# A diffusion-transformer step: the filler matmuls of the delta-rule scan redistributed, an activation reload split into four awaited groups, and the down-projection's operand loads cut into pieces

## The chip, the cores and the metric

The kernel runs on one core of one Trainium2 chip. The metric is the device time in microseconds (us) of one execution. Three executions of the kernel before gave 2773.88, 2765.34 and 2752.76 us, median 2765.34 us.

## The reference

One trunk layer of a hybrid backbone, in float32, for 256 context tokens and 1024 latent tokens (1280 together, `T`), width 1024:

- `h = RMSNorm(x) * g * (1 + scale) + shift`, with shift, scale and gate from `SiLU(cond) @ w_ada + b_ada`.
- The in-projection `h @ w_in` (1024 to 4896 columns) gives attention q, k, v, the inputs of a gated delta net (q, k, v, z, beta, alpha) and two gates.
- Attention: 8 query heads, 2 key heads, softmax over context, cached and latent keys.
- Delta net: conv, SiLU, then for each of 8 heads a forward and a backward scan in chunks: `S_t = a_t (I - b_t k_t k_t^T) S_{t-1} + b_t k_t v_t^T`, `o_t = S_t^T q_t`. In a chunk a triangular matrix is inverted.
- `x = x + gate1 * W_o(sig(ga) * W_pa(attention) + sig(gb) * W_pb(delta))`.
- `x = x + gate2 * W_down(SiLU(h2 @ W_gate) * (h2 @ W_up))`, with 2816 hidden columns.

Every output is compared in float32, so each large product is made of three matmuls on a high and a low part of both factors: high·high, low·high and high·low.

## The kernel before, in words

The program is a sequence of blocks, one after the other, each with a hand-written order for every engine and with semaphores between the engines: modulation and norm, in-projection, delta scan, keys, attention, merge, and feed-forward. The change touches the delta scan and the last part of the feed-forward.

**Delta scan (`delta_scan`, line 751).** A unit is one chunk of 128 tokens in one direction. Units 0 to 19 alternate forward and backward. The loop runs over u from -3 to 20: in step u the engines invert unit u's matrix, carry the state of unit u-1, and prepare units u+1 to u+3. Below, "unit u" is the stretch of that step. The matrix is inverted in three levels (`LV`); between its small matmuls lie 13 slots, 0 to 12. On TensorE slot 0 follows the first level's `bank_A` products, slots 1 and 2 its `banks_bc` products, slots 3 to 5 and 6 to 8 stand alike in levels two and three, and slots 9 to 12 in the two closing products.

Into the slots go **fillers**: 960 matmuls of 128x320 (`bank_F`, line 1209) that finish the in-projection. They make 10 tiles for the first 640 tokens and then the same 10 for the other 640, 48 matmuls a tile, in two groups of 24 (8 slices k of the width, three parts). `quota` says how many go into a slot: 4, but 2 in unit -2, and none in units -3 and 8. So the fillers run from unit -2 to slot 2 of unit 18. A filler group ends with a copy by ACT (`fill_out`); weights are split by ACT and DVE when a tile starts.

Between the tenth and the eleventh tile the activations `h_hi` and `h_lo` (8 slices each, 320 KB a slice) are overwritten with the other half of the tokens, by 16 DMAs from `h_late` in SP's queue. `reload` (line 902) issues four of them at four places of a unit: at the end of unit RELOAD-1, after its `blocks_in`, then in unit RELOAD at its start, after `inverse_in`, and after `blocks_out`. TensorE waits for all 16 (`h2_in` >= 256) before the first filler of tile 10, in slot 0 of unit 9.

SP's order in a unit: load decays and the reload's part, load `kv`, then `inverse_out` (waits for the small diagonal inverse of the next unit) and `inverse_in` (16 DMAs), the reload's next part, `kq`, `blocks_out` (8 DMAs), the reload's next part, the store of o, `blocks_in`. Stores of filler tiles and loads of their weights lie between. DVE begins each unit with `Y` (line 1173) and the state's step, and then works through the diagonal blocks (lines 1156 to 1165), for which it needs what `blocks_in` brought, before it makes the second level's `Y`; the `attn_t` products (line 1133) follow.

**Down-projection (`feed_forward`, line 2541).** After the gate and up products (22 steps, f stored to `f_t` in DRAM), 56 steps u = 0 to 55 compute the down-projection by Strassen-like products: 2 halves of tokens (h), 7 products (j), 4 row tiles (p), u = 28h + 4j + p, 33 matmuls of 128x320 each (line 3045). A step needs a split weight slot: SP loads `down_raw` (704 KB, two buffers), ACT makes the high part, DVE the low part (`down_high`, `down_low`, four slots). A product needs a split operand in three pieces (k 0 to 3, 4 to 7, 8 to 10), made by `f_sum`, `f_high` and `f_low` from four quadrants of f, `quad["11"]` to `quad["22"]`, 1760 KB each. Each quadrant is one DMA for a half of the tokens (`load_quad`, line 2626): for the first half 11 and 12 in the steps FT and FT+1 of the up stage, 22 and 21 after its end, ahead of the weights of u = 2 to 4. For the second half 11, 12 and 22 are issued together at u = 20, and 21 at u = 24. SP's loop also loads weights five steps ahead, and loads and stores the residual rows; it is one in-order queue.

## Time and profile before

| | |
|---|---|
| three executions | 2773.88, 2765.34, 2752.76 us (median 2765.34) |
| profiled execution | 2758.34 us, its span 2756.5 us |
| mean granted TensorE clock | 0.956 |
| TensorE busy | 2533.8 us (92%), 17286 matmuls |
| VectorE / ScalarE / GpSimd busy | 1712.2 (62%) / 1224.0 (44%) / 614.1 us (22%) |
| DMA | 357.63 MB, mean 130 GB/s |
| delta scan, from the warm-up to its last state | 555 to 1237 us |
| down-projection | 2458.5 to 2753.6 us |

The time is that of a chain in which TensorE is nearly always the engine at work, so it is read by asking where TensorE idles or runs at the lower clock. A window's row has for each engine the busy us and the instructions, then the granted TensorE clock as a share of full speed, the share of DMA time and the GB/s. In a timeline the bracket gives the idle time just before the instruction and what ended it. Units of the scan are told apart by TensorE's first `bank_A<-x_base` product: unit 1 begins at 627.7 us, unit 5 at 753.9, unit 7 at 814.6, unit 8 at 851.0, unit 9 at 881.0, unit 10 at 924.0, unit 11 at 955.3, unit 18 at 1165.5, unit 19 at 1190.5, unit 20 at 1220.7.

### The profile page before, as it was taken

The numbers are of one execution on the slowest core, as the hardware profiler recorded it, in microseconds if no ns is written. First come the engines' busy times: TensorE is split into PE (matmuls) and PEld (weight loads), VectorE is DVE, ScalarE is ACT, GpSimd is POOL, SyncE is SP. The second block draws the span as 40 slices with busy tenths as digits, with TensorE's granted clock in tenths as the row PEclk, the third lists the DMA queues.
The fourth block names the chain that finished last, engine by engine and source line by source line (L and its number), as shares of the span: only waits on it lengthen the run. The fifth ranks groups of instructions, "written<-read, shape, count | busy, mean of one in ns | idle before, by whom it ended". The sixth has DMA issues, their size and how long they took to land. (4 is left out here: it accounts for less than half of the span.)

```text
span 2756.5 us, 45691 instructions
## 1 busy us (share of the span) xinstructions
PE 2533.8 (92%) x17286; PEld 2382.0 (86%) x17286; DVE 1712.2 (62%) x2811; ACT 1224.0 (44%) x2201; POOL 614.1 (22%) x547
## 2 busy tenths in 40 slices
PE   6999999969998999983999988989999999989999
PEld 2899999958887888972888878989999999989899
DVE  3666333146766676746888883457886655757676
ACT  4322333234333344314888883354653333535343
POOL 1000222243433334305344453232000000000000
PEclk9999999979997999966999999999999999999999
DMA  5322666343345333315001005543335542445854
GB/s 217 138 86 95 203 216 214 115 132 96 103 115 154 91 92 99 80 40 193 11 18 56 18 17 175 201 152 109 113 112 193 186 149 106 153 148 186 289 171 150
DMA packets 237936, 357.63 MB, mean 130 GB/s; under 512 B 85888, under 2 KB 161696, under 8 KB 236192
## 3 DMA queue, kind: packets, MB, share of 16 engines
q1 hardware_dynamic: 234848, 339.11, 37.6%
q10 hardware_dynamic: 2880, 15.73, 1.7%
q8 instruction: 133, 2.18, 0.3%
q14 instruction: 75, 0.61, 0.1%
HBM read 262.66 MB, written 92.09 MB: 129 GB/s over the span
## 5 line engine op out<-in xcount | busy, mean ns | idle before, releaser
L277 PE MATMUL proj_ps<-h_hi,w_hi 128*128 128x320 f32 x896 | 283.0, 316 | 6.0 <-DVE w_lo L571 5.6
L277 PE MATMUL proj_ps<-h_hi,w_lo 128*128 128x320 f32 x896 | 278.3, 311 | 0.0
L277 PE MATMUL proj_ps<-h_lo,w_hi 128*128 128x320 f32 x896 | 278.3, 311 | 0.0
L1075 ACT ACTIVATE x_inv<-banks_bc 128x1024 fp32r<-128x1024 f32 x120 | 122.6, 1025 | 271.4 <-PE banks_bc L1209 270.4
L2243 DVE TENSOR_TENSOR mf_up_slots<-mf_up_raw,mf_up_slots 128x512 fp32r<-128x512 f32 x198 | 137.3, 694 | 115.5 <-ACT mf_up_slots L2218 115.2
L277 PEld LDWEIGHTS proj_ps<-h_hi,w_hi 128*128 128x128 f32 x896 | 169.8, 189 | 7.1 <-DVE w_lo L571 3.3
L277 PEld LDWEIGHTS proj_ps<-h_lo,w_hi 128*128 128x128 f32 x896 | 169.9, 190 | 0.0
L277 PEld LDWEIGHTS proj_ps<-h_hi,w_lo 128*128 128x128 f32 x896 | 169.6, 189 | 0.0
L3006 PE MATMUL f_ps_b<-mf_t_r,mf_up_slots 128*128 128x320 f32 x1056 | 166.1, 309 | 3.2 <-DVE mf_sg L2921 3.2
L3006 PE MATMUL f_ps_b<-mf_t_s,mf_up_slots 128*128 128x320 f32 x1056 | 165.7, 309 | 2.0 <-PEq L2248 2.0
L3006 PE MATMUL f_ps_c<-mf_t_s,mf_up_slots 128*128 128x320 f32 x1056 | 165.6, 309 | 0.0
L3006 PEld LDWEIGHTS f_ps_b<-mf_t_r,mf_up_slots 128*128 128x128 f32 x1056 | 157.3, 188 | 4.7 <-issue 4.2
L420 POOL TENSOR_TENSOR w_ada_lo<-w_ada_raw,w_ada_hi 128x2048 fp32r<-128x2048 f32 x16 | 73.9, 4616 | 388.4 <-ACT w_ada_hi L424 388.4
L3006 PEld LDWEIGHTS f_ps_b<-mf_t_s,mf_up_slots 128*128 128x128 f32 x1056 | 157.5, 188 | 2.3 <-DVE mf_up_slots L2243 2.2
L3006 PEld LDWEIGHTS f_ps_c<-mf_t_s,mf_up_slots 128*128 128x128 f32 x1056 | 157.6, 188 | 0.0
L2015 DVE TENSOR_TENSOR t_exps_lo<-t_t_ps,t_exps_hi 128x512 fp32r<-128x512 f32 x200 | 137.8, 689 | 30.2 <-ACT t_exps_hi L1836 27.0
L3045 PE MATMUL f_ps_b<-mf_f_operand,mf_down_slot 128*128 128x320 f32 x924 | 139.9, 312 | 9.5 <-DVE mf_down_slot L2867 9.5
L3045 PEld LDWEIGHTS f_ps_b<-mf_f_operand,mf_down_slot 128*128 128x128 f32 x924 | 138.0, 190 | 9.7 <-DVE mf_down_slot L2867 9.7
L2002 DVE TENSOR_REDUCE t_block_max<-t_s_ps 128x1 f32<-128x512 f32 x192 | 130.6, 680 | 8.4 <-PE t_s_ps L1782 8.0
L2561 ACT ACTIVATE mf_down_slot<-mf_down_raw 128x1408 fp32r<-128x1408 f32 x56 | 77.2, 1379 | 129.8 <-PE f_ps_b L3045 35.5
L1862 ACT ACTIVATE t_exps<-t_s_ps,t_neg_max 128x512 f32<-128x512 f32 x192 | 130.8, 682 | 9.0 <-DVE t_neg_max L2005 9.0
L2218 ACT ACTIVATE mf_up_slots<-mf_up_raw 128x512 fp32r<-128x512 f32 x198 | 120.6, 625 | 31.5 <-DVE mf_up_raw L2236 17.2
(387 smaller groups left out, 6884.9 us busy)
## 6 DMA issues: line engine op xcount, KB each, us to landing
mf_up_raw<-w_up_dram SPq DMA_DIRECT2D x33, 1024.0 KB, 5.0
w_raw<-w_in_dram SPq DMA_DIRECT2D x48, 512.0 KB, 4.4
mf_down_raw<-down_sums SPq DMA_DIRECT2D x32, 704.0 KB, 4.1
mf_down_raw<-w_down_dram SPq DMA_DIRECT2D x24, 704.0 KB, 4.3
w_ada_raw<-w_ada_dram SPq DMA_DIRECT2D x16, 1024.0 KB, 5.1
mf_w_raw<-w_mix_dram SPq DMA_DIRECT2D x30, 512.0 KB, 5.0
f_t<-mf_c SPq DMA_DIRECT2D x44, 320.0 KB, 2.4
mf_f_quad<-f_t SPq DMA_DIRECT2D x8, 1760.0 KB, 10.6
```

The lines of the kernel that those rows point to most:

```text
L277: ins = nc.tensor.matmul(out, w(k), a(k), start=(first and n == 0 and q == 0), stop=(last and n == len(ks) - 1 and q == 2))
L420: nc.gpsimd.tensor_tensor(wl[:], wr[:], wh[:].bitcast(F32), ALU.subtract).then_inc(ada_lo, 1)
L1075: nc.scalar.activation(XX[:, c].rearrange("p t h i -> p t (h i)"), BC[c][:], ACT.Copy).then_inc(e["x_ready"], 1)
L1862: last = nc.scalar.activation(pf[:, x % SLOTS], s_ps[x % SBANKS][:], ACT.Exp, bias=negm[:, u % UR, a:a + 1], accum_out=sm[:, u % UR, a, b: ...
L2002: nc.vector.tensor_reduce(pmax[:, u % UR, a, b:b + 1], s_ps[x % SBANKS][:], AX_X, ALU.max).then_inc(e["block_maxed"], 1)
L2015: nc.vector.tensor_tensor(pl[:, p % HL], t_ps[p % 2][:], ph[:, p % HL].bitcast(F32), ALU.subtract).then_inc(e["lo_ready"], 1)
L2218: self.nc.scalar.activation(self.slot(q, 0), self.source(q), ACT.Copy).then_inc(self.hi_ready, 1)
L2243: self.nc.vector.tensor_tensor(self.slot(q, 1), self.source(q), self.slot(q, 0).bitcast(F32), ALU.subtract).then_inc(self.lo_ready, 1)
L2561: cp = lambda o, s: nc.scalar.activation(o, s, ACT.Copy)
L3006: last = nc.tensor.matmul(out[:, 0:GN], up.slot(q, wp)[:, k], t_operand(w, t, PRODUCTS[i], tp)[:, k], start=(i in (0, 1, 3) and k == 0 and ...
L3045: last = nc.tensor.matmul(bank[:, 0:GN], slot[:, wp, k], operand[J % 2][:, fp, k], start=(fresh and k == 0 and part == 0), stop=(k == F_HA ...
```

## The change

- **Fillers.** 2 a slot in unit -3, 3 in unit -2, 4 in units -1 to 1, 3 in units 2 to 14, 4 from unit 15 on. The tenth tile ends in slot 9 of unit 8. Unit 9 has none in slots 0 to 5 and 3 in slots 6 to 12. The last filler moves from slot 2 of unit 18 to slot 0 of unit 20. The sum stays 960: units 2 to 6 and 10 to 14 have 39 where they had 52, unit 8 has 30 for none, unit 9 has 21 for 52, unit 18 has 52 for 12, unit 19 has 52 for none, unit 20 has 4.
- **Reload.** RELOAD is 9, so the four groups are issued one unit later: at the end of unit 8, at the start of unit 9, after its `inverse_in`, after its `blocks_out`. SP waits before each group but the first until the one before has landed. TensorE waits for one group at a time, before slices 0, 2, 4 and 6 of tile 10's first group of matmuls, in slots 6, 8, 10 and 12 of unit 9.
- **Down-projection.** Each quadrant load becomes three DMAs, by the pieces (640, 640 and 480 KB), each after the first waiting for the one before. ACT and DVE wait for a piece. For the first half, 11 and 12 come over the steps FT to FT+2; 22 and 21 move behind the first weights, one piece a step at u = 1 to 6. For the second half they come one piece a step from u = 20 to 31, in the order 11, 12, 22, 21. The weights of u = 2 are issued ahead of the last store of f, those of 3 and 4 right after it, `load_rows(1)` at u = 4.

```
-        RELOAD = 8
-        def quota(u):
-            return {-3: 0, -2: 2, RELOAD: 0}.get(u, 4)
+        RELOAD = 9
+        def quota(u, s):
+            if u == RELOAD:
+                return 0 if s < SLOTS // 2 else 3
+            return {-3: 2, -2: 3}.get(u, 3 if 2 <= u < RELOAD + 6 else 4)
...
                     if n == 0:
                         sp.wait_ge(e["fill_ps"], 2 * FILL_TILES)
+                    else:
+                        sp.wait_ge(e["h2_in"], 64 * n)
...
-                        if t == FILL_TILES:
-                            pe.wait_ge(e["h2_in"], 256)
...
                         k, part = divmod(i, 3)
+                        if t == FILL_TILES and g == 0 and part == 0 and k % 2 == 0:
+                            pe.wait_ge(e["h2_in"], 64 * (k // 2) + 64)
...
+        quad_no = lambda half, c: 16 * (3 * half + c + 1)
+        QUADS_AT = {(0, 0, 1): ("22", 0), (0, 0, 2): ("22", 1), (0, 0, 3): ("22", 2), (0, 1, 0): ("21", 0), (0, 1, 1): ("21", 1), (0, 1, 2): ("21", 2),
+                    (0, 5, 0): ("11", 0), (0, 5, 1): ("11", 1), (0, 5, 2): ("11", 2), (0, 5, 3): ("12", 0), (0, 6, 0): ("12", 1), (0, 6, 1): ("12", 2),
+                    (0, 6, 2): ("22", 0), (0, 6, 3): ("22", 1), (1, 0, 0): ("22", 2), (1, 0, 1): ("21", 0), (1, 0, 2): ("21", 1), (1, 0, 3): ("21", 2)}
...
-            def load_quad(half, name):
+            def load_quad(half, name, c):
                 a, g = int(name[0]) - 1, int(name[1]) - 1
+                lo, hi = PIECES[c]
+                if c:
+                    sp.wait_ge(q_in[name], quad_no(half, c - 1))
+                sp.dma_start(quad[name][:, lo:hi], io["f_t"][F_HALF * a + lo:F_HALF * a + hi, :, half * HT + g * GN:half * HT + g * GN + GN].rearrange("k p n -> p k n")).then_inc(q_in[name], 16)
...
             load_down(1)
+            load_down(2)
             store_f(N - 1)
-            sp.wait_ge(prod, len(index))
-            load_quad(0, "22")
-            load_quad(0, "21")
+            load_down(3)
             sp.wait_ge(f_out[1], 16 * FT)
-            for u in range(2, 5):
-                load_down(u)
-            for G in range(2):
-                load_rows(G)
+            load_down(4)
+            load_rows(0)
             for u in range(ND):
...
                 load_down(u + 5)
-                if h == 0 and (j, p) == (5, 0):
-                    sp.wait_ge(t_sum, sum_no(0, "22", 2))
-                    load_quad(1, "11")
...
+                if (h, j, p) in QUADS_AT:
+                    name, c = QUADS_AT[h, j, p]
+                    if h == 0 and j < 2:
+                        sp.wait_ge(prod, len(index))
+                    elif name == "11":
+                        sp.wait_ge(t_sum, sum_no(0, "22", c))
+                    else:
+                        sp.wait_ge(t_lo, ready(0, {"12": "s3", "22": "s4", "21": "22"}[name], c))
+                    load_quad(1 if j > 4 else h, name, c)
+                if u == 4:
+                    load_rows(1)
```

## Rows read from the trace of the kernel before

**Rows 1.** Windows, one stretch to a row: warm-up, units 1, 5, 8, 9, 10, 11 to 17, 18, 19.
```profile
555.00:600.10 45.10, 24.46 (x108) 19.55 (x108) 16.26 (x36) 16.33 (x38) 29.04 (x29) 0.65 0.48 128
627.70:660.80 33.10, 31.27 (x224) 29.17 (x223) 21.10 (x44) 12.41 (x21) 13.47 (x12) 0.90 0.36 95
753.90:784.70 30.80, 28.80 (x224) 26.69 (x223) 21.83 (x44) 13.64 (x23) 12.55 (x11) 1.00 0.37 109
851.00:881.00 30.00, 26.31 (x172) 24.08 (x172) 21.27 (x43) 11.33 (x19) 11.78 (x11) 0.77 0.59 186
881.00:924.00 43.00, 36.12 (x225) 34.20 (x225) 23.13 (x46) 12.26 (x21) 13.63 (x12) 0.76 0.38 112
924.00:955.30 31.30, 28.89 (x225) 26.62 (x224) 22.04 (x43) 12.54 (x22) 12.20 (x11) 1.00 0.38 100
955.30:1165.50 210.20, 199.90 (x1556) 186.37 (x1555) 150.28 (x302) 82.83 (x137) 79.87 (x65) 1.00 0.36 98
1165.50:1190.50 25.00, 22.08 (x168) 21.12 (x167) 18.06 (x35) 7.20 (x9) 5.23 (x5) 0.93 0.24 63
1190.50:1220.70 30.20, 28.92 (x155) 28.34 (x155) 10.37 (x18) 6.14 (x6) 1.48 (x2) 0.60 0.04 15
```

**Rows 2.** Timeline of TensorE in units 1 and 5: start us, us, then [idle before <-releaser].
```profile
638.31 0.33 PE L1209 MATMUL banks_bc<-y_res,x_inv 128*128 128x128 f32 x1 [1.52 <-DVE y_res L1173]
...
763.39 0.33 PE L1209 MATMUL banks_bc<-y_res,x_inv 128*128 128x128 f32 x1 [0.40 <-DVE y_res L1173]
...
765.92 1.13 PE L1209 MATMUL bank_A<-kq_t 64*128 64x256 f32 x8
...
768.89 1.32 PE L1209 MATMUL bank_A<-x_inv,n_t_eye 128*128 128x128 f32 x8 [1.06 <-DVE attn_t L1133]
```

**Rows 3.** Windows (columns as in Rows 1), half clock after the wait in unit 9.
```profile
884.80:905.20 20.40, 15.82 (x70) 15.85 (x70) 9.85 (x22) 3.07 (x3) 1.95 (x2) 0.50 0.43 146
```

**Rows 4.** Timeline of the SP queue, end of unit 8.
```profile
868.38 7.48 SPq L895 DMA_DIRECT2D x_base<-diag_inv  x16
...
883.88 0.43 SPq L908 DMA_DIRECT2D h_lo<-h_late  x1
```

**Rows 5.** Timeline of TensorE, unit 9.
```profile
889.38 0.60 PE L1209 MATMUL bank_F<-h_hi,w_hi 128*128 128x320 f32 x1 [6.37 <-issue]
```

**Rows 6.** Timeline of TensorE in the down-projection.
```profile
2458.52 5.00 PE L3045 MATMUL f_ps_a<-mf_f_operand,mf_down_slot 128*128 128x320 f32 x33
...
2463.36 5.00 PE L3045 MATMUL f_ps_c<-mf_f_operand,mf_down_slot 128*128 128x320 f32 x33
...
2511.77 5.00 PE L3045 MATMUL f_ps_a<-mf_f_operand,mf_down_slot 128*128 128x320 f32 x33
...
2589.21 3.68 PE L3045 MATMUL f_ps_a<-mf_f_operand,mf_down_slot 128*128 128x320 f32 x24
...
2599.57 2.77 PE L3045 MATMUL f_ps_a<-mf_f_operand,mf_down_slot 128*128 128x320 f32 x9 [6.68 <-DVE mf_f_operand L2848]
...
2743.84 9.84 PE L3045 MATMUL f_ps_b<-mf_f_operand,mf_down_slot 128*128 128x320 f32 x66
```

**Rows 7.** Timeline of SP, ACT and DVE in the down-projection.
```profile
2460.40 1.30 SPq L2628 DMA_DIRECT2D mf_f_quad<-f_t  x2
...
2474.74 1.38 ACT L2561 ACTIVATE mf_down_slot<-mf_down_raw 128x1408 fp32r<-128x1408 f32 x1 [14.32 <-DMA mf_down_raw<-w_down_dram]
...
2476.15 3.33 DVE L2867 TENSOR_TENSOR mf_down_slot<-mf_down_raw,mf_down_slot 128x1408 fp32r<-128x1408 f32 x2 [14.07 <-ACT mf_down_slot L2561]
...
2573.55 8.08 SPq L2628 DMA_DIRECT2D mf_f_quad<-f_t  x3
```

**Rows 8.** Windows (columns as in Rows 1), around the second stall.
```profile
2580.00:2600.00 20.00, 13.32 (x89) 13.05 (x89) 7.98 (x10) 5.89 (x5) 0.00 (x0) 0.87 0.98 341
```

**Rows 9.** DMA issues: operation, count, KB each, median us from issue to landing.
```profile
mf_down_raw<-w_down_dram SPq DMA_DIRECT2D x24, 704.0 KB, 4.3
...
mf_f_quad<-f_t SPq DMA_DIRECT2D x8, 1760.0 KB, 10.6
```

More of the change, by code:

```diff
@@ L847, in delta_scan @@
                 t, i = divmod(at[0], PER)
-                n = min(quota(u), 3 * KT - i % (3 * KT))
+                n = min(quota(u, s), 3 * KT - i % (3 * KT))
                 pieces[u, s] = []
@@ L2624, in store_f @@
                     sp.dma_start(io["f_t"][f, :, tok(t)], c1[t][:]).then_inc(f_out[t], 16)
-            def load_quad(half, name):
+            def load_quad(half, name, c):
                 a, g = int(name[0]) - 1, int(name[1]) - 1
-                sp.dma_start(quad[name][:], io["f_t"][F_HALF * a:F_HALF * a + F_HALF, :, half * HT + g * GN:half * HT + g * GN + GN].rearrange("k p n -> p k n")).then_inc(q_in[name], 16)
+                lo, hi = PIECES[c]
+                if c:
+                    sp.wait_ge(q_in[name], quad_no(half, c - 1))
+                sp.dma_start(quad[name][:, lo:hi], io["f_t"][F_HALF * a + lo:F_HALF * a + hi, :, half * HT + g * GN:half * HT + g * GN + GN].rearrange("k p n -> p k n")).then_inc(q_in[name], 16)
             def load_down(u):
@@ L2698, in _ @@
                     sp.wait_ge(f_out[0], 16 * FT)
-                    load_quad(0, "11")
+                    for c in range(2):
+                        load_quad(0, "11", c)
                 if n == FT + 1:
-                    load_quad(0, "12")
+                    load_quad(0, "11", 2)
+                    load_quad(0, "12", 0)
                     load_down(0)
+                if n == FT + 2:
+                    for c in range(1, 3):
+                        load_quad(0, "12", c)
             load_down(1)
+            load_down(2)
             store_f(N - 1)
-            sp.wait_ge(prod, len(index))
-            load_quad(0, "22")
-            load_quad(0, "21")
+            load_down(3)
             sp.wait_ge(f_out[1], 16 * FT)
-            for u in range(2, 5):
-                load_down(u)
-            for G in range(2):
-                load_rows(G)
+            load_down(4)
+            load_rows(0)
             for u in range(ND):
@@ L2717, in _ @@
                 load_down(u + 5)
-                if h == 0 and (j, p) == (5, 0):
-                    sp.wait_ge(t_sum, sum_no(0, "22", 2))
-                    load_quad(1, "11")
-                    sp.wait_ge(t_lo, ready(0, "s3", 2))
-                    load_quad(1, "12")
-                    sp.wait_ge(t_lo, ready(0, "s4", 2))
-                    load_quad(1, "22")
-                if h == 0 and (j, p) == (6, 0):
-                    sp.wait_ge(t_lo, ready(0, "22", 2))
-                    load_quad(1, "21")
+                if (h, j, p) in QUADS_AT:
[9 more added lines that the diff above has]
+                    load_rows(1)
                 if p == 2 and j in (4, 5, 6) or p == 2 and j == 0 and h:
@@ L2747, in f_high @@
                 else:
-                    act.wait_ge(q_in[{"11": "11", "12": "21", "s4": "22"}[name]], 16 * half + 16)
+                    act.wait_ge(q_in[{"11": "11", "12": "21", "s4": "22"}[name]], quad_no(half, c))
                 if J == 1:
@@ L2758, in down_high @@
                     if u == 0:
-                        act.wait_ge(q_in["11"], 16)
+                        act.wait_ge(q_in["11"], quad_no(0, 0))
                     elif u < 4:
@@ L2854, in f_sum @@
                 if name == "s1":
-                    dve.wait_ge(q_in["12"], 16 * half + 16)
+                    dve.wait_ge(q_in["12"], quad_no(half, c))
                 if name == "s2":
-                    dve.wait_ge(q_in["22"], 16 * half + 16)
+                    dve.wait_ge(q_in["22"], quad_no(half, c))
                 if name == "s3":
```

## The prediction, made before the changed kernel was run

> **What bounds the kernel now.** I read the page's busy times first. TensorE is busy 92% of the span, so only its idle time, its low clock, and work that could lie in such time are for sale. The windows then say where that is.
>
> The delta scan first [rows 1]. Units 11 to 17, all with 52 fillers, take 210.2 us, 30.0 each, at clock 1.00. Unit 9 takes 43.0 at 0.76. Unit 8, with no filler, still takes 30.0 at 0.77, and unit 19, with no filler and no preparation of later units, 30.2 at 0.60. So a unit without fillers isn't short: TensorE falls to half clock, and what was saved is lost. Inside a full unit [rows 2] TensorE waits twice for DVE: 0.40 us at 763.39 for `y_res`, behind the diagonal blocks, and 1.06 us at 768.89 for `attn_t`. The unit has 30.8 - 28.8 = 2.0 us of idle in all, 1.46 in these two waits; so from the second wait to the end at 784.7 the stretch is TensorE's own.
>
> The reload: TensorE stops 6.37 us at 889.38 [rows 5] and then runs at 0.50 of full clock, the 1.2 GHz level, until 905.2 [rows 3]. What it waits for is late because of SP's order: the 16 `x_base` DMAs hold the queue from 868.38 to 875.86, and the last reload DMA goes out at 883.88 [rows 4], 5.5 us before the fillers start.
>
> In the down-projection [rows 6] one step of 33 matmuls takes 2463.36 - 2458.52 = 4.84 us, 0.147 us a matmul. Steps 0 to 7 take 2511.77 - 2458.52 = 53.25 us against 8 x 4.84 = 38.72, so 14.5 are lost; steps 24 to 53 take 2743.84 - 2589.21 = 154.63 against 145.20, so 9.4 are lost. Between, nothing is. Both losses begin at a queue of large loads [rows 7]: two quadrants issued at 2460.40 ahead of the weights, for which ACT then waits 14.32 us, and three issued from 2573.55, after which TensorE waits 6.68 us in step 24, with the DMA engines at 0.98 and 341 GB/s [rows 8].
>
> **The change part by part.** The sum is made against the profiled execution, 2758.3 us (span 2756.5 and 1.8 around it), which is 7.0 below the median of the runs.
>
> *Units with 39 fillers for 52 (2 to 6 and 10 to 14).* Thirteen matmuls are 1.9 us. The six of them in slots 0 to 5 lie ahead of the two DVE waits, which only grow, by up to 0.9. The seven in slots 6 to 12 lie in TensorE's own stretch: 7 x 0.147 = 1.0 us. Bounds 0 and 1.9 a unit; I take 1.0, as the DVE chain up to `attn_t` doesn't contain a filler. Units 2 to 6 and 11 to 14: -9.3. SP's loop through diagonal blocks is nearly as long as a unit, so more than 1.9 can't come.
>
> *Unit 7* has 39 fillers for 40: 0. Its state's output stays where it is in SP's queue. *Unit 8* gets 30. With the clock held it should be a 39-filler unit (29.0) less its last 9 fillers, which lie in TensorE's stretch (-0.4 net of the low clock that may begin there): 28.6, so -1.4. If the clock falls as now, +2.
>
> *Units 9 and 10.* By unit 8's rows SP reaches the third group 25 us after the unit's start (875.86 less 851.0), that group lands some 5.5 us after its last DMA, at 32, and only then does SP issue the fourth, which lands at about 38 to 39. TensorE reaches slot 10 at about 29 and slot 12 at about 35. So the reload isn't hidden: two waits of about 3 us take the place of one of 6.4, and unit 9 is about 39.3 for 43.0. The low clock then falls into unit 10: 29.0 + 4 = 33.0 for 31.3. Together -2.0, bounds -12 (all hidden) and +6 (the longer waits come out as 5 and 6, with the low clock of unit 9 behind them). SP standing in its new waits has `kv` (a unit of slack), `inverse_out` (due only at 15 us) and `blocks_in` of the next unit behind it; the last is issued at about 36 us and needed at 43, so it holds.
>
> *Units 18 to 20.* Unit 18: it was 25.0 with 12 fillers; a full unit without those two groups of products is about 27.2: +2.2. Unit 19 at full clock with 52 fillers: busy time of unit 5, 28.8, less 2.1 for its two groups of products (1.13 us a group at 765.92, a little of it overlapped) [rows 2], 26.7, for 30.2: -3.5. Four fillers in unit 20 lie in its waits: 0. *Warm-up*: TensorE is busy 24.5 of 45.1 us there [rows 1] and bound by others' chains; 36 more fillers cost 5 to 10 us inside those waits: 0, and +3 if the first products slip.
>
> *Clock.* Nothing above pays for new dips. In unit 1 a wait of 1.52 us at 638.31 [rows 2] was enough for one: 33.1 us at 0.90 against 30.0 [rows 1], a price of 3.1. The waits for DVE grow to about 1.0 and 1.4, so I allow for one more such dip: +3. The Trainium skill, page "TensorE: Matmul & The Clock Gate", section "A second HAM failure mode: psum-queue depth-cycling", tells of a kernel whose matmul groups are parted by short idles often enough that the clock oscillates; by it fewer fillers are a danger and not a gain, which is the third rival below. Unit 1 agrees with it, units 11 to 17 don't.
>
> Scan: -9.3 - 1.4 - 2.0 - 1.3 + 3 = **-11**.
>
> *Down-projection, first half.* With the quadrants behind, the weights of step 2 go out at about 2457 and those of 3 to 6 follow, each when a low part is done. A load takes 4.3 us [rows 9], ACT's part 1.4, DVE's 1.6, and sums and low parts of an operand's pieces about as much by their size (an estimate from 1.67 us for 1408 elements a row) [rows 7]. From 2460.4, DVE then has the low parts of weights 1 to 6, three sums and three low parts before step 4 has its third piece: twelve, some of them shorter, and a wait or two for a load, until about 2482.6. TensorE wants it at 2481.5, so about 1 us is left of 14.5. *Second half*: pieces of 11 are in from step 22 on and needed at 28; 12 likewise. But steps 20 to 27 now ask for 704 + 600 + 160 + 160 KB each (weights, piece, rows in and out), 1.66 MB in 4.84 us or 344 GB/s, just what the busiest row gives (341). Loads are issued three to five steps ahead, so I let 1 to 2 us show. Gain 24.0 less 2.5: **-21**, bounds -24 and -12.
>
> The pieces are 16 more DMAs, each landing on its own; a 704 KB load lands in 4.3 us and a 1760 KB one in 10.6 [rows 9], so three pieces are no slower in sum and the first is there 6 us sooner. The Trainium skill, page "DMA: Bandwidth & Descriptors", section "Bandwidth", says to batch copies to 1 MiB or more. By it pieces of 480 to 640 KB waste time on the engines just where these are full, and the term would come nearer its -12. No row of this trace has such a piece alone.
>
> Sum: -11 - 21 = -32, so 2726 for the profiled execution and **2734 us** for the median.
>
> **The rivals.** One per cent is 27.7 us (about what this kernel's runs tell from no change), so the line to faster is 2737.6, close to the forecast.
>
> 1. *Both parts come out at their good end*: the clock holds, the reload is hidden, no stall in the down-projection. -20 - 24 = -44, about 2721. For it: unit 5 has a wait of 1.06 us at clock 1.00. Against: SP's order in unit 9. Chance 0.15.
> 2. *The down-projection becomes a matter of DMA*: steps 20 to 31, and 1 to 6, run at the transfers' pace, and only half of its loss is regained. -11 - 12 = -23, 2742. For: 344 against 341 GB/s. Against: steps 28 to 31 ask for less, and slots run four ahead. Chance 0.13.
> 3. *The clock dips in about every third unit with 39 fillers*: 10 units, 3 more dips of 3.1, and the reload's low clock in full. Scan -11 + 9 + 4 = +2; total -19, 2746. For: unit 1, and units 8 and 19. Against: units 11 to 17 at 1.00. Chance 0.20.
> 4. *Slower: the clock stays low through most of the thinned units.* Unit 19 shows the price: without fillers or products its work is 28.8 - 7.6 - 2.1 = 19.1 us at full clock, and it was busy 28.9 at 0.60, half as much again. A 39-filler unit (26.9 busy) would so take 40, 10 more than now; ten units: +100. It decides from the point where it holds in six of the ten: +60, less 5 for what is left of the scan's gain, less 21, is +34, 2799. Against: three fillers still part the small products in every slot, where units 8 and 19 had none. Chance 0.04.
> 5. *The change doesn't do what it says*: the fillers stay in the way (0 a unit) and the second half's pieces come no sooner. About -14, 2751. Chance 0.03.
>
> **How the numbers follow.** The forecast has 0.45, from 2725 to 2745, a little over half of it beyond the line: 0.30 faster, 0.15 same. With rival 1 (all faster) 0.45; rivals 2, 3 and 5 are within 1%, with a few hundredths of 2 beyond the line: faster 0.48, same 0.48, slower 0.04. The range goes from rival 1's end with the runs' own scatter, 2716, to rivals 3 and 5, 2756; outside is rival 4 and the tails.
>
> **What would show it.** Units 11 to 14 at 29.0 us and clock 1.00; unit 19 at 27 with clock near 1; in unit 9 two idles of TensorE for the second half of the reload, about 3 us each, and no stop at slot 0; unit 10 at 33. In the down-projection `f_ps_a` of step 8 at about 40 us after step 0, no idle of 6 us at step 24, and DMA rows near 340 GB/s for steps 20 to 27. I am wrong on the first count if thinned units remain at 30 with longer DVE waits, on the second if TensorE idles for `mf_down_slot` after step 20.

## The result and the profile after

| | us | interval or range |
|---|---|---|
| before, median of 15 runs | 2760.97 | 2751.16 to 2773.88 |
| changed, median of 15 runs | 2740.34 | 2734.26 to 2747.36 |
| ratio changed to before | 0.9926 | 0.9911 to 0.994 |
| profiled execution, before / changed | 2758.34 / 2741.12 | spans 2756.5 / 2739.3 |

The change takes 20.6 us off the median and 17.2 us off the profiled execution. The forecast was 2734, which is 31 us under the 2765.34 of the three executions known then; the median of fifteen is 4.4 us lower than that. The kernel is faster by three quarters of a per cent, clear of its interval, but short of the one per cent that the forecast drew as its line. All of the gain comes from one half of the change.

**Down-projection.** Its first matmuls start at 2463.65 and its last two steps end at 2726.65 + 9.84 = 2736.5, 272.8 us; before they took 295.1 [rows 6]. That is 22.3 less, where 21 was forecast. TensorE's timeline of the changed kernel (start us, us, operation, [idle before <-releaser]):

```profile
2463.65 5.00 PE L3059 MATMUL f_ps_a<-mf_f_operand,mf_down_slot 128*128 128x320 f32 x33
...
2487.05 1.59 PE L3059 MATMUL f_ps_a<-mf_f_operand,mf_down_slot 128*128 128x320 f32 x9 [0.35 <-DVE mf_f_operand L2862]
...
2503.00 3.68 PE L3059 MATMUL f_ps_a<-mf_f_operand,mf_down_slot 128*128 128x320 f32 x24
2507.31 1.58 PE L3059 MATMUL f_ps_a<-mf_f_operand,mf_down_slot 128*128 128x320 f32 x9 [0.63 <-DVE mf_f_operand L2862]
...
2581.45 5.00 PE L3059 MATMUL f_ps_a<-mf_f_operand,mf_down_slot 128*128 128x320 f32 x33
...
2726.65 9.84 PE L3059 MATMUL f_ps_b<-mf_f_operand,mf_down_slot 128*128 128x320 f32 x66
```

Step 8 begins 39.35 us after step 0 (53.25 before); step 24, at 2581.45, has all its 33 matmuls in one run. Where 14.5 and 9.4 us were lost before, two idles of 0.35 and 0.63 us are left, both in front of the third piece of an operand.

**Delta scan.** It was to give 11 us and gives nothing: the first matmul of the next block (`k_ps`) starts at 1242.79, before at 1240.88. Windows of the changed kernel (stretch, length, busy time and instructions of PE, PEld, DVE, ACT, POOL, granted clock, DMA share, GB/s): warm-up, units 0, 5, 8, 9, 10, 11 to 14, 15 to 17, 18, 19. They answer to [rows 1].

```profile
555.00:602.40 47.40, 30.82 (x145) 26.57 (x143) 18.09 (x37) 17.20 (x40) 27.23 (x27) 0.73 0.48 136
602.40:639.50 37.10, 34.58 (x167) 32.16 (x168) 16.56 (x36) 12.37 (x21) 11.04 (x9) 0.59 0.34 95
762.40:792.20 29.80, 26.78 (x211) 24.76 (x211) 22.23 (x44) 12.39 (x21) 11.56 (x10) 1.00 0.37 105
855.10:884.00 28.90, 27.08 (x202) 25.03 (x201) 19.57 (x41) 11.42 (x20) 11.30 (x10) 0.94 0.31 79
884.00:926.10 42.10, 32.10 (x193) 29.37 (x193) 23.60 (x46) 11.43 (x19) 17.15 (x15) 0.78 0.69 218
926.10:956.60 30.50, 29.19 (x211) 27.43 (x211) 20.82 (x43) 12.51 (x21) 6.81 (x5) 0.91 0.22 57
956.60:1083.00 126.40, 116.35 (x837) 107.29 (x837) 85.70 (x172) 47.96 (x81) 50.48 (x43) 0.92 0.35 97
1083.00:1173.20 90.20, 85.52 (x668) 79.95 (x667) 66.30 (x130) 34.07 (x54) 29.04 (x25) 1.00 0.34 94
1173.20:1199.40 26.20, 25.65 (x209) 25.09 (x207) 19.04 (x36) 8.72 (x11) 5.02 (x5) 1.00 0.21 53
1199.40:1227.60 28.20, 27.30 (x220) 26.58 (x218) 12.39 (x20) 7.24 (x9) 3.67 (x4) 1.00 0.07 25
```

And the same of the kernel before, for two stretches not shown yet, unit 0 and units 11 to 14:

```profile
600.10:627.70 27.60, 26.38 (x167) 24.34 (x168) 16.48 (x36) 12.29 (x21) 7.89 (x8) 0.85 0.41 116
955.30:1076.50 121.20, 114.36 (x890) 106.48 (x889) 86.59 (x174) 49.60 (x84) 51.07 (x41) 1.00 0.39 110
```

Unit 0 is 9.5 us longer, at clock 0.59 for 0.85. Units 11 to 14 have 52 fillers less in all and are 5.2 us longer, at 0.92 for 1.00. Unit 19 is shorter: from its start to the last update of the state it is 36.2 us, 43.2 before. Gains and losses of much the same size lie on top of each other. ("To the last update" means to the start of the last `bank_S<-v_new,k_decayed` matmuls.)

### The profile page after: what moved, and what is told of

Same layout as the page of the kernel before. It is cut to its first block and busy times, and to the rows that moved or that the text cites. A ratio compares the mean times of both kernels' runs of the same rounds, so it can differ in the third digit from the quotient of the medians.

```text
span 2739.3 us, 45719 instructions
## 1 busy us (share of the span) xinstructions
PE 2531.5 (92%) x17286; PEld 2379.8 (87%) x17286; DVE 1717.3 (63%) x2811; ACT 1224.1 (45%) x2201; POOL 611.1 (22%) x547
## 5 line engine op out<-in xcount | busy, mean ns | idle before, releaser
L1213 PE MATMUL bank_F<-h_hi,w_hi 128*128 128x320 f32 x320 | 122.1, 382 | 15.9 <-DMA h_lo<-h_late 7.1
```

What stands on the lines that cost most here:

```text
L1213: mm = lambda o, a, b, st=True, sp_=True: nc.tensor.matmul(o, a, b, start=st, stop=sp_)
```

## The experiments

All twelve were timed, each beside the kernel before on the same chip; each ratio is to those runs. They ran on four chips, whose medians of the kernel before lie between 2761.67 and 2763.74 us, so a difference between the medians of two experiments is less sure than a ratio by some 2 us. Each experiment has one profile. To sum the scan up I take a unit's length as the distance between the first `x_base` products of two units. A *thinned* unit has 39 fillers for 52, a *fall* is a stretch in which the granted clock is 0.5, the 1.2 GHz level.

**1 and 2: one half of the change each.** First the scan of before with the new down-projection (of the diff, everything from `quad_no` on):

```
-        RELOAD = 9
+        RELOAD = 8
...
```

> The kernel before with the down-projection part of the change alone; fillers and reload as before. Theory A (the whole gain is the down-projection, the scan part gives nothing): 21 to 24 us under the kernel before, so at or slightly under the changed kernel's 20.6. Theory B (the scan part does give some of its forecast 11 us, and the down-projection less than its 21): 10 to 15 us under. In the trace both want steps 0 to 55 to take some 272 to 273 us where they took 295, and unit lengths as before.

Then the new scan with the old down-projection (of the diff, everything ahead of `quad_no`):

```
-            def load_quad(half, name, c):
+            def load_quad(half, name):
...
```

> The kernel before with the fillers and the reload of the change alone; down-projection as before. Theory A (39-filler units are not shorter, because TensorE's clock falls for a moment after the 1.4 us wait for attn_t): within 5 us of the kernel before, and dips of the clock about 15 us into the thinned units again. Theory B (the dips of the one profiled run were chance): 8 to 12 us under.

The down-projection alone: 2736.06 us, ratio 0.991 [0.9889, 0.993]. The scan alone: 2761.36, ratio 0.9989 [0.9976, 1.0002]. So the down-projection is the change, and the scan's part is worth nothing that can be measured: by the first it would cost about 4 us (0.9926 against 0.991), by the second it would give 1.5, and the intervals allow both.

**3: four fillers again behind the reload**

```
-            return {-3: 2, -2: 3}.get(u, 3 if 2 <= u < RELOAD + 6 else 4)
+            return {-3: 2, -2: 3}.get(u, 3 if 2 <= u < RELOAD else 4)
```

> The changed kernel, but 4 fillers a slot again in units 10 to 14 (3 in units 2 to 8 and in the second half of 9); the fillers then end in unit 18. Theory A (3 a slot lets the clock fall): units 11 to 14 at 30.0 us and clock 1.00, as long as or shorter than the changed kernel's 31.0, 33.8, 31.4, 30.3, while units 3 to 8 still dip; but unit 19, without fillers, falls to half clock and takes 30 again, so the time is within 4 us of the changed kernel. Theory B (the dips have another cause, for example their place in the run): dips in units 11 to 14 too.

2741.56 us, ratio 0.9936 [0.9911, 0.996], the same as the changed kernel. But the clock behaves otherwise: of units 11 to 17, now with 52 fillers, six stay at full clock at 29.6 to 30.8 us and one (unit 13, 32.0) doesn't, while of units 2 to 8, still thinned, all but unit 5 fall. Thinning brings the falls, and what it saves they take. The other half of the expectation failed: unit 19, here without fillers, doesn't take 30 us but 22.2, at clock 0.92.

```profile
1199.00:1221.20 22.20, 20.18 (x154) 19.39 (x154) 11.15 (x18) 5.82 (x6) 2.04 (x2) 0.92 0.09 35
```

From unit 19's start to the last update of the state it is 36.9 us, 36.2 in the changed kernel and 43.2 before. So most of what the last units gained comes without any filler in unit 19; what this kernel shares with the changed one is a full unit 18 (44 and 52 fillers, 12 before).

This can be counted over four profiles with the changed scan (the changed kernel, experiments 2, 5 and 6), units 2 to 6 and 11 to 14, and two with the old one (before and experiment 1), units 2 to 6 and 11 to 17:

| units | no fall | one of 3.4 us | longer falls | mean |
|---|---|---|---|---|
| 39 fillers, 36 units | 6, 29.2 us | 23, 30.9 us | 7, 33.8 us | 31.2 us |
| 52 fillers, 24 units | 21, 30.1 us | 3, 31.9 us | 0 | 30.3 us |

The other profiles say the same, less sharply. With unit 7 of these and the evenly thinned units of experiments 3, 7, 8 and 9 (units 8 to 10 left out) there are 74 thinned units: 55 fall, mean 30.9 us. With the full units (50 to 52 fillers) of the rest there are 65: 13 fall, mean 30.5 us. So thinning doesn't pay, but its loss is 0.9 us a unit in the table and only 0.4 over all.

Of the 30 falls in the table 23 come behind one wait, that for `attn_t`; five come behind a wait for `y_res` (in the changed kernel those of units 11 and 12, behind 1.87 and 1.88 us), two earlier still. In the changed kernel's units 2 and 3:

```profile
685.71 1.32 PE L1213 MATMUL bank_A<-x_inv,n_t_eye 128*128 128x128 f32 x8 [1.37 <-DVE attn_t L1137]
...
714.99 1.32 PE L1213 MATMUL bank_A<-x_inv,n_t_eye 128*128 128x128 f32 x8 [1.38 <-DVE attn_t L1137]
```

Unit 2 had the same wait and no fall (29.6 us); in unit 3 (30.9 us) the granted clock is 0.5 for 3.4 us from 716.7 on, 1.7 us behind it. So the wait alone doesn't decide. It decides how often, though. These are all units 2 to 7 and 11 to 17 (without experiment 11, and without unit 7 of the old scan), the unevenly filled ones of experiments 4, 10 and 12 among them, by their longest wait for `y_res` or `attn_t` in the first 17.5 us; each field has falls of units:

| longest wait | full units | evenly thinned | unevenly thinned |
|---|---|---|---|
| up to 1.14 us | 3 of 48 | 3 of 3 | 1 of 18 |
| 1.30 to 1.41 us | 0 of 1 | 37 of 56 | none |
| 1.53 us and more | 10 of 16 | 15 of 15 | 9 of 10 |

Two of the three thinned units of the first row, and the unevenly thinned one, fell before either wait. A full unit with a long wait falls too, and the kernel before has one, unit 2 (32.0 us):

```profile
675.81 1.72 PE L1209 MATMUL bank_A<-x_inv,n_t_eye 128*128 128x128 f32 x8 [1.73 <-DVE attn_t L1133]
```

So it is the length of the wait that goes with the falls, and the number of fillers by way of it: 52 fillers leave 1.06 us in this place [rows 2], 39 leave 1.37.

**4: the 39 fillers placed unevenly**

```
+            if 2 <= u < RELOAD + 6:
+                return (3, 3, 3, 4, 5, 6, 3, 2, 2, 2, 2, 2, 2)[s]
...
```

> The changed kernel with the same 39 fillers a thinned unit (2 to 8, 10 to 14) placed otherwise: 3, 3, 3, 4, 5, 6 in slots 0 to 5, ahead of TensorE's two waits for DVE, and 3, 2, 2, 2, 2, 2, 2 in slots 6 to 12. Theory A (what costs is the idle time ahead of attn_t, which drops the clock): that wait shrinks from 1.4 to about 0.5 us, the dips behind it go, the thinned units take about 28.5 to 29 us, and the time is 10 to 20 us under the changed kernel. Theory C (what holds the clock is the fillers' own share of the work, wherever they lie): the dips move to slots 6 to 12, units stay at 30 to 31, same time. Theory D (units are bound by SP's loop through the diagonal blocks): clock 1.00 but units at 29.5 to 30, with longer waits of DVE for diag_blocks.

2733.67 us, ratio 0.9891 [0.9868, 0.9914]: 6.7 us under the changed kernel by the medians, less than the 10 to 20 expected. The wait before the middle of the unit shrinks:

```profile
683.44 1.32 PE L1215 MATMUL bank_A<-x_inv,n_t_eye 128*128 128x128 f32 x8 [0.41 <-DVE attn_t L1139]
```

This unit takes 27.6 us at full clock. Over three profiles with this placing (4, 10 and 12, units 8 to 10 beside the reload left out) 18 of 28 units have no fall and take 28.8 us; 5 take 31.2 and 5 take 33.4; the mean is 30.0. So the fillers ahead of DVE's late results hold the clock more often than those behind them. How much time that is worth stays unsure: 0.9 us a unit against all evenly thinned units, but experiment 10, which differs from 9 in this placing, takes 271.1 for 272.4 us over the nine thinned units away from the reload.

**5 and 6: one half of the down-projection each.** Experiment 5 keeps the pieces and the new order for the first half's operands and loads the second half's whole, where before; 6 does the reverse.

```
+                if h == 0 and (j, p) == (5, 0):
+                    sp.wait_ge(t_sum, sum_no(0, "22", 2))
+                    load_whole(1, "11")
...
```

and experiment 6:

```
             load_down(1)
-            load_down(2)
             store_f(N - 1)
+            sp.wait_ge(prod, len(index))
+            load_whole(0, "22")
+            load_whole(0, "21")
...
```

> The changed kernel, with the second half of the down-projection's operands loaded as before: one load for each quadrant, all at step 20 and 24, each behind the whole of what it replaces. What stays of the change there is the first half: the quadrants 22 and 21 behind the first down weights, in pieces. Theory A (the two halves give their gains by themselves, 14.5 us from the first half's two stalls and 9.5 us from step 24's): this kernel loses about 9 us against the changed one, some 2749 us, and TensorE waits 5 to 7 us at step 24 as before, and not at steps 4 and 8. Rival C (the order of the first half is what gives both, since it also lets the rows and the weights of later steps come earlier): the wait at step 24 is gone here too, 2741 us. Rival D (the first half's gain comes back at step 24): TensorE waits 10 us or more there and the time is 2755 us.

> The changed kernel, with the first half of the down-projection's operands loaded as before: 11, 12, 22 and 21 whole, 22 and 21 ahead of the down weights of step 2 and later. The second half stays in pieces, each behind the piece that it replaces. Theory A (each half by itself): the stalls of some 6.4 and 4.4 us at the first steps and at step 8 come back, with the slower steps around them, in all 12 to 15 us, so about 2754 us, and no wait at step 24. Rival C (the pieces alone give most of it): under 2745 us. Rival D (a late first half pushes the loads of the second half later too): a wait at step 24 as well, 2760 us.

2751.37 us, ratio 0.9963 [0.995, 0.9977], and 2752.53, ratio 0.9981 [0.9959, 1.0003]. From the first step to the start of the last pair it is 285.3 us before [rows 6], 263.0 changed, 270.7 in experiment 5 and 275.6 in 6: the first half alone gives 14.6 us and the second alone 9.7, where the forecast had losses of 14.5 and 9.4. Together they would be 24.3; 22.3 were measured, so they are independent but for 2 us. TensorE in 5, at step 24, and in 6, at step 2:

```profile
2592.74 2.77 PE L3066 MATMUL f_ps_a<-mf_f_operand,mf_down_slot 128*128 128x320 f32 x9 [6.63 <-DVE mf_f_operand L2869]
```
```profile
2477.05 12.64 PE L3056 MATMUL f_ps_b<-mf_f_operand,mf_down_slot 128*128 128x320 f32 x66 [9.38 <-DVE mf_down_slot L2878]
```

The wait of 6.63 is the 6.68 of [rows 6]. Experiment 6 has no wait at step 24. The 66 matmuls behind its stall took 12.64 us for 9.84, at a granted clock of 0.76: the clock fell there too.

**7: the activations reloaded by columns**

```
+            def reload(g):
+                sp.wait_ge(e["fill_ps"], 2 * FILL_TILES - 1 + g)
+                for part, h in enumerate((h_hi, h_lo)):
+                    cols = slice(g * GN, (g + 1) * GN)
+                    sp.dma_start(h[:, :, cols].bitcast(F32), io["h_late"][part][:, :, cols]).then_inc(e[("h2_in", "h3_in")[g]], 16)
...
```

> The changed kernel, with the activations of the fillers reloaded by columns instead of rows: the columns that the first product group of a filler tile reads are reloaded as soon as the tenth tile's first group is done, the others when its second group is done. So 24 fillers lie between a reload's issue and its first reader, nothing is paused, and unit 9 has its three fillers in each place as its neighbours have (the quota of three now holds up to unit 16, so that the sum is the same). Theory A (unit 9 is 42 us long because of its two waits of 3.8 and 3.4 us and of the half clock that follows a stretch without fillers): unit 9 comes down to 30 or 31 us, the waits on the reload are gone, units 15 and 16 stay near 30 us, and the time falls by 10 to 13 us against the changed kernel, to 2727 to 2731 us. Rival C (the reload's 5.2 MB crowd the scan's own transfers wherever they lie): unit 9 or 10 keeps 5 us or more of it in waits for x_base or the diagonal blocks, 2735 us or more. Rival D (the clock falls in the thinned units at random and takes the gain): k_ps no earlier than 1240 us, 2740 us.

2746.39 us, ratio 0.9954 [0.9938, 0.997]: no gain, rather a loss against the changed kernel. The waits for the reload are gone, but unit 9 is 43.1 us long. SP, DVE and TensorE in it:

```profile
888.17 0.53 SPq L903 DMA_DIRECT2D h_hi<-h_late  x1
888.74 0.73 SPq L903 DMA_DIRECT2D h_lo<-h_late  x1
...
891.73 0.48 SPq L880 DMA_DIRECT2D diag_blocks<-diag  x1
...
901.55 0.16 DVE L1149 COPY diag_inverse<-diag_blocks 64x2 f32<-64x2 f32 x1 [9.84 <-DMA diag_blocks<-diag]
...
905.42 0.48 PE L1202 MATMUL banks_bc<-y_res,x_inv 128*128 128x128 f32 x1 [9.55 <-DVE y_res L1166]
```

The 64 KB of `diag_blocks` went out 3 us behind 2.5 MB of activations (with a store and 512 KB of weights between) and came 9.8 us later. DVE stood in that wait with `y_res` behind it, and TensorE behind that. The reload's cost isn't only in its own waits; it makes the scan's small transfers late, as rival C had it.

**8: the old warm-up**

```
-            return {-3: 2, -2: 3}.get(u, 3 if 2 <= u < RELOAD + 6 else 4)
+            return {-3: 0, -2: 2}.get(u, 3 if 5 <= u < RELOAD + 6 else 4)
```

> The changed kernel with the fillers of before in the warm-up (none in the first unit, two in the second) and four in each place up to unit 4, so that the sum ahead of the reload is enough; units 5 to 8 and 10 to 14 stay thinned. Theory A (fillers in the first unit of the warm-up delay the first products by 6.5 us and leave the clock low for 20 to 31 us of unit 0, against 10 to 20 us before): the first products start near 562 us, unit 0 is 28 to 32 us long and not 33 to 37, and k_ps comes 4 to 8 us earlier, 2733 to 2737 us. Rival C (unit 0's low clock has nothing to do with the warm-up's fillers and differs from run to run): unit 0 is as long as in the changed kernel, the time within 3 us of it. The chance I give A is 0.5.

2732.05 us, ratio 0.9897 [0.9873, 0.992], and `k_ps` 11.8 us earlier than in the changed kernel's profile. Units 2 to 4 have 52 fillers here and take the same as thinned (91.5 us; 91.7 changed). The difference is ahead of them. Seven profiles with fillers in the first unit of the warm-up and four a place in units 0 and 1 (changed, 2 to 7) start unit 0 at 601.3 us in the mean and take 66.7 to 71.0 us for units 0 and 1, mean 68.4. Six without (before, 1, 8, 9, 10, 12) start at 599.0 and take 59.5 to 65.5, mean 63.5. So the new warm-up costs 2.3 + 4.9 = 7.2 us. The starts of unit 0 overlap (599.3 is the earliest of the seven, 600.2 the latest of the six), the lengths of units 0 and 1 don't, by 1.2 us.

**9 to 11: the column reload in eight pieces**

```
+            def reload(g, j):
+                sp.wait_ge(e["fill_ps"], 2 * FILL_TILES - 1 + g)
+                if 4 * g + j:
+                    sp.wait_ge(e["h2_in"], 32 * (4 * g + j))
...
+            return {-3: 0, -2: 2}.get(u, 3 if 5 <= u < 17 else 4)
```

Experiment 10 has `(3, 3, 3, 4, 5, 6, 3, 2, 2, 2, 2, 2, 2)[s]` for the three of units 5 to 16, experiment 11 has `(3, 3, 3, 5, 6, 6, 4, 3, 2, 2, 2, 2, 3)[s]` from unit 0 on.

> The kernel with the old warm-up (2732 us), with the activations reloaded by columns as in the run before, but in eight pieces of 0.65 MB, one for every six fillers, each issued behind the landing of the one before and 24 fillers ahead of its first reader; three fillers in each place of units 5 to 16, four elsewhere. Theory A (unit 9 of the run before lost 9.6 us because the 64 KB of diag_blocks landed 9.8 us after issue, behind 2.5 MB of activations in the queue; in small pieces it lands in about 3 us): VectorE's wait for diag_blocks in units 8 to 10 stays under 2 us, unit 9 is 30 to 32 us long instead of 43.5, and the time is 2719 to 2724 us. Rival C (any reload traffic of 5 MB in these units costs the scan the same in sum): units 8, 9 and 10 are together over 96 us and the time is 2727 us or more. Rival D (the clock falls after the waits in the thinned units and takes 2 or 3 us in most of units 5 to 16): k_ps comes less than 6 us ahead of the 1231.0 us of the kernel with the old warm-up.

> The kernel of the run with spaced pieces, with the 39 fillers of units 5 to 16 placed unevenly: 3, 3, 3, 4, 5, 6, 3 and six times 2, so that more of them lie ahead of the waits for y_res and attn_t. Theory A (TensorE waits less before the middle of a unit, so that the clock falls there in fewer units): 8 or more of the 12 thinned units without a fall, at 27.5 to 29 us each, and 6 to 10 us less than with even placing. Rival C (the falls only move to the first third of the unit, where few fillers are left, and last 7 to 10 us there, as in units 3, 5 and 11 of the placed kernel before): within 4 us of even placing.

> The kernel of the run with spaced pieces, with 44 fillers in every unit from 0 to 19, placed 3, 3, 3, 5, 6, 6, 4, 3, 2, 2, 2, 2, 3, so that no unit is thinned to 39 and none has 52. Theory A: units of 28 to 29 us nearly throughout, the clock at full speed in most of them; 2710 to 2716 us, the fastest kernel here. Rival C (three fillers in the first places instead of four lower the clock in units 0 and 1, as in the kernel with placed fillers): units 0 and 1 together 66 us or more instead of 59.5, and no gain over the other placing. Rival D (units 18 and 19 with fewer fillers lose what the change gained there): the stretch from unit 19 to the last state is over 40 us instead of 36.

2745.06 us (0.993 [0.9905, 0.9956]), 2730.65 (0.9885 [0.9861, 0.9909]) and 2736.72 (0.991 [0.9888, 0.9931]). Experiment 10 is level with the kernel with the old warm-up (2732.05), the other two are slower. Experiment 9's theory A on the reload's size fell: unit 9 is 46.7 us long. SP and DVE in it:

```profile
886.61 0.47 SPq L913 DMA_DIRECT2D h_lo<-h_late  x1
891.35 0.36 SPq L913 DMA_DIRECT2D h_hi<-h_late  x1
891.76 0.47 SPq L913 DMA_DIRECT2D h_lo<-h_late  x1
892.27 0.48 SPq L888 DMA_DIRECT2D diag_blocks<-diag  x1
...
897.27 0.16 DVE L1159 COPY diag_inverse<-diag_blocks 64x2 f32<-64x2 f32 x1 [16.18 <-DMA diag_blocks<-diag]
```

SP itself stood from 887.1 to 891.3: what its program has there is the wait for the landing of the pair before, and that pair's second load landed at 891.29, 4.7 us after its issue. `diag_blocks` came behind the next pair. It then landed 5 us after its issue, but DVE had waited 16.18. What counts is the place in the queue, of the transfer and of SP's own waits, and not the size of the pieces. Placed against even fillers (10 against 9) is 14.4 us, more than the 6 to 10 expected; part of it is unit 9 (42.9 against 46.7), so this pair of times doesn't price the placing alone. In experiment 10 seven of the 12 thinned units have no fall, where 8 or more were expected. Experiment 11 missed its 2710 to 2716 by 20 us: the stall moved to unit 10 (43.3 us), and of the other units 1 to 17 six have a fall, five of them at a wait for `y_res` of 1.39 to 2.81 us.

**12: the reload right behind `diag_blocks`**

```
                 if has(u + 2):
                     blocks_in(u + 2)
+                if u in (8, 9):
+                    reload(u - 8)
...
+            if u == 8:
+                return -(-(PER * FILL_TILES - 3 * KT - at[0]) // (SLOTS - s))
+            if u == 9:
+                return 4 if s < 6 else 2
+            if u == 10:
+                return 2 if s < 5 else 4
```

> The kernel with the old warm-up, the activations reloaded by columns in two whole parts of 2.5 MB, each issued right behind the load of diag_blocks at the end of units 8 and 9, the one place of SyncE's queue after which nothing that the scan waits for is issued for some 10 us. The fillers are planned for it: the tenth tile's first group ends with unit 8, its second in the sixth place of unit 9, two in each place from there to the fifth place of unit 10; units 2 to 7 and 11 to 13 have their fillers placed 3, 3, 3, 4, 5, 6, 3 and six times 2. Theory A (the 9.8 us and 16.2 us that VectorE waited for diag_blocks in the two kernels reloaded by columns were its place behind the activations, and the wait on an earlier piece, in the queue): no wait for diag_blocks over 3 us in units 8 to 10, no wait of TensorE over 3 us there, units 9 and 10 together 62 to 66 us and not 74 as with the old warm-up, and a time of 2718 to 2726 us, the fastest kernel here. Rival C (the rows of the next decay and of kv_rows, now behind the activations, are late in their turn): a wait of 3 us or more on one of them in unit 9 or 10 and 2730 us or more. Rival D (two fillers in a place are too few and the clock stays low over half of units 9 and 10): both over 35 us, no gain.

2715.85 us (2711.18 to 2717.89), ratio 0.9835 [0.981, 0.986]: a little better than expected, 24.5 us under the changed kernel, and the fastest kernel here. SP at the end of its unit 9, with DVE and TensorE, which are in unit 10 by then:

```profile
904.38 0.48 SPq L888 DMA_DIRECT2D diag_blocks<-diag  x1
904.90 0.60 SPq L911 DMA_DIRECT2D h_hi<-h_late  x1
905.54 0.67 SPq L911 DMA_DIRECT2D h_lo<-h_late  x1
...
906.55 0.16 DVE L1157 COPY diag_inverse<-diag_blocks 64x2 f32<-64x2 f32 x1 [2.80 <-DMA diag_blocks<-diag]
...
910.42 0.33 PE L1210 MATMUL banks_bc<-y_res,x_inv 128*128 128x128 f32 x1 [2.43 <-DVE y_res L1174]
```

and its windows of units 8, 9 and 10:

```profile
843.15:872.00 28.85, 27.49 (x218) 25.73 (x217) 22.42 (x44) 11.96 (x20) 12.03 (x11) 1.00 0.36 100
872.00:899.75 27.75, 26.34 (x210) 24.58 (x209) 21.93 (x43) 12.40 (x21) 11.95 (x10) 1.00 0.58 182
899.75:932.70 32.95, 29.88 (x215) 27.73 (x214) 20.75 (x44) 12.51 (x21) 12.49 (x11) 0.90 0.59 177
```

Units 9 and 10 take 60.7 us for 72.5 changed, though they hold 80 fillers for 60, with no wait for the activations; the same bytes are moved. The kernel differs from the others in the fillers of these units too, so the 11.9 us aren't the price of the place in the queue alone; what the traces show of the place is DVE's wait for `diag_blocks`, 2.80 us for 9.84 and 16.18. Of the 23.3 us by which `k_ps` comes earlier than in the changed kernel's profile, these two units are 11.9, the warm-up with units 0 and 1 is 5.8, units 2 to 8 with their placed fillers 6.2 and units 11 to 14 are 5.9. Units 15 to 19 give 6.4 back, 3.6 of it in units 16 and 17, where the clock falls with 52 fillers behind waits of 1.85 and 1.72 us.

## Why the prediction was right in time and half right in its reasons

The time came out 6 us over the forecast, the gain at two thirds of it: 20.6 us for 31. Luck has a share. The warm-up with units 0 and 1 (9.9 us) and the thinned units (11.4) cost more than the sum had for them, and 9.9 us that the sum didn't have came back in units 7 and 8 (5.4) and from unit 18 on (4.5).

- **Down-projection, -21 forecast, -22.3 measured: right**, by its two stalls, and experiments 5 and 6 show each alone. Of the first I left 1 us, 0.98 is there. The 1 to 2 us kept back for the DMA engines weren't needed: from 2562 to 2600, some eight steps from step 20 on, they were at a share of 0.88 and 288 GB/s, and TensorE was busy for all of the 38.00 us. I had set a demand of 344 GB/s as if every step had all four transfers; the loads run ahead and spread it. The pieces of 640 KB landed in 6.2 us in the median. By the Trainium skill, page "DMA: Bandwidth & Descriptors", section "Bandwidth", copies under 1 MiB cost efficiency; that this would bring the term near -12 the trace refutes, since what counts here is when the first piece is there. Whether the engines lose efficiency isn't shown: 288 GB/s at a share of 0.88 make 327 at a full one, 341 at 0.98 [rows 8] make 348 (an estimate, from stretches that carry different loads).
- **The thinned units, -9.3 with +3 for one dip: the step that failed.** The waits grew as I worked out (1.37 us for `attn_t`, "about 1.4"), and a unit whose clock held takes 29.2 us where I had 29.0. But "Nothing above pays for new dips" and one allowed dip were wrong: 30 of 36 thinned units had one. Each is cheaper than the 3.1 us that I read from unit 1, 30.9 - 29.2 = 1.7 us for the common one, but a unit without a fall gains only 30.1 - 29.2 = 0.9 by thinning. Mean 31.2 against 30.3: a loss of 0.9 a unit (0.4 over all profiles). This is the third rival's mechanism, at 5 units in 6 instead of 1 in 3. That the scan's sum is the +2 it named is chance: the warm-up's 9.9 us and what came back from unit 7 on aren't in that rival. The Trainium skill, page "TensorE: Matmul & The Clock Gate", section "A second HAM failure mode: psum-queue depth-cycling", told of groups parted by short idles and a clock that oscillates; the traces of the thinned units agree. I had weighed it against units 11 to 17, which all had 52 fillers, and had overlooked unit 2 of the same trace, full, with a wait of 1.73 us for `attn_t` and a fall behind it.
- **Warm-up, 0 with "+3 if the first products slip": wrong.** They slipped from 562.03 to 568.54, and unit 0 ran at low clock from 604.0 to 634.7 us. Over the profiles it is 7.2 us. I looked only for a wait in which 36 fillers fit, and not at what comes behind them in TensorE's order.
- **Unit 7, 0: wrong to the good.** Units 7 and 8 take 59.7 us, 66.5 before. Before, TensorE waited 3.67 us for `y_res` at 827.33, behind 4.50 us in which DVE waited for `diag_blocks`: SP had issued that 4.7 us into unit 7, right behind a store and 512 KB of weights. In the changed kernel these two go out in unit 6, and `diag_blocks` 1.9 us into unit 7. The price is a wait of 2.52 us for `attn_t` in unit 6, which is 2.4 us longer. It is experiment 7's mechanism in small, and it stood in the old trace. No run isolates it, but unit 7 takes 36.4 and 34.7 us in the two profiles with the old scan and 29.1 to 30.8 in the four with the changed one.
- **Units 9 and 10, -2.0: right in kind, -1.7 in the pair of profiles.** There are two waits, forecast at about 3 us each:

```profile
917.31 0.41 PE L1213 MATMUL bank_F<-h_hi,w_hi 128*128 128x320 f32 x1 [3.78 <-DMA h_lo<-h_late]
...
925.15 0.64 PE L1213 MATMUL bank_F<-h_hi,w_hi 128*128 128x320 f32 x1 [3.35 <-DMA h_lo<-h_late]
```

  But unit 9 is 42.1 us and not 39.3, and unit 10 30.5 and not 33.0: the low clock lay in unit 9, with waits of 1.03 and 0.94 us in its first half. And the old side is less sure than one profile made it look: in experiment 1, with the scan of before, unit 8 is 35.9 us, unit 9 32.0, and the wait of 6.37 us [rows 5] is 0.56. Units 7 to 10 take 140.7 us before, 132.2 changed and 132.4 in experiment 1, so that against the second profile of the old scan units 7 and 8 gain 10.9 us, 9 and 10 lose 10.7, and the four together give nothing.
- **Units 18 and 19, -1.3: too small.** Unit 18 +1.2 for +2.2; from unit 19's start to the last state -7.0 for -3.5. The clock held to the end of the unit, 1.00 for 0.60, and the last unit's chain behind it gained as well. The fillers of unit 19, which I had taken for the cause, are hardly needed for it: experiment 3 has none there and gains 6.3 of the 7.0 us to the last update. Its empty unit 19 of 22.2 us also answers "a unit without fillers isn't short", which I had read from units 8 and 19; that holds where the clock falls, and behind a full unit 18 it did so for 3.4 us only.

In sum the scan is +1.9: start of unit 0 +2.2, units 0 and 1 +7.7, units 2 to 6 -0.1, 7 and 8 -6.8, 9 and 10 -1.7, 11 to 14 +5.2, 15 to 17 +1.2, 18 +1.2, 19 to `k_ps` -7.0. The 3.2 us between `k_ps` and the down-projection aren't the change's: over the fourteen profiles this stretch, in code that nobody touched, takes 1217.6 to 1223.9 us.

Still open: why some units with the same waits keep the clock and others don't (19 of 56 at 1.30 to 1.41 us), why unit 0's low clock lasts from 7 to 31 us, and what in unit 18 keeps the clock of unit 19.

## What to carry to other kernels

Work that fills an engine's idle time does most just ahead of the waits that it can't avoid: taken from there, it made the waits longer, and the clock took back what was saved. Before a bulk transfer is moved or cut up, list the small transfers that someone waits for behind it in the same queue, and SP's own waits ahead of them: units 9 and 10 took 60.7 us with the same 5 MB in one place of the queue and 71.7 to 78.0 in the eleven profiles that have them in other places of these units. A sum read from one profiled execution should be compared with a second one where a stall is near its cover; a wait of 6.4 us was 0.6 in the next.

## What was not expected of the hardware

- Of 57 units with a longest wait of 1.30 to 1.41 us between groups of small matmuls 37 had a fall to half clock, of 3.4 us each; of 69 with at most 1.14 us 7 had one, of 41 with 1.53 us or more 34.
- A 64 KB load landed 9.8 us after its issue with 2.5 MB of older loads in its queue, and 2.1 and 2.4 us after it when issued ahead of them.
